# Paired attention in a two-block transformer kernel, with the gather schedule spread anew

## The chip, the cores and the metric

The kernel runs on one core of one Trainium2 chip. The metric is device time in microseconds for one execution of the whole program, as the median of three runs. Everything is in fp32. Engines are named as in the profile: PE is TensorE (PEld its weight load), DVE is VectorE, ACT is ScalarE, POOL is GpSimd, SP issues the weight transfers.

## The reference, cut to what matters

Two transformer blocks over 512 tokens (plus 16 meta tokens in the first) of width 1024. The first block has a latent attention (8 heads, q and k 96 wide, v 64) beside a retention branch, then an expert layer ("PEER"): per token 128 experts are chosen from 16384, their rows of `peer_u` are multiplied with the token and their rows of `peer_v` are summed with the resulting weights. The second block has a pooling branch beside an attention with 16 heads in 2 key groups and three branches per head, then an up/down MLP.

```python
# first block, per tile i of 128 queries
s = jnp.einsum('bhqd,bhkd->bhqk', qb, k) * scale
s = jnp.where(kpos[None, :] <= qpos[:, None], s, -jnp.inf)
o = jnp.einsum('bhqk,bhkd->bhqd', jax.nn.softmax(s, axis=-1), v)
# experts
act = jax.nn.gelu(jnp.einsum('td,tkd->tk', xt, peer_u[it]))
y = jnp.einsum('tk,tkd->td', gt * act, peer_v[it])
# second block, per head: compressed keys, selected blocks, window
o = gb[..., 0:1] * o_c + gb[..., 1:2] * o_s + gb[..., 2:3] * o_w
```

With 512 tokens the selection takes all blocks and the window covers everything, so both full branches are plain causal attention over `128 (t + 1)` keys for query tile t; the compressed branch has 15 keys after two tiles, 31 after four, with a mask of its own.

## The kernel before, in words

The 512 tokens are four tiles of 128 rows. Each block runs in two waves of two tiles: `first_wave` with run 0 (tiles 0, 1) and run 1 (tiles 2, 3), then `second_wave` with run 0 and run 1. Run by run the stages follow each other; a stage's tag with the run behind it is its name here. In the first block: n1 (norm), lat, nq, nkv, up, qk, tq, tk (transposes of q and k), the attention ma0 (run 0: tiles 0 and 1 in one stage) or ma2 and ma3 (run 1: tile 3 has 528 keys and a stage of its own), rp, tr, re, rn (retention), to (transposes of the attention's output), m1, mix, np, pq, and sel0 to sel3 (choice of the experts, VectorE work). In the second: n2, u, pool, q, kc, kv, cmp (the compressed keys), tq, tk, the attention na, to, m, out, n3, ff1, ff2, nf.

**Stages.** Each stage writes its instructions to all engines; an engine's queue is in order, and `Core.begin` makes each wait for the last results of the stage before. Weights stream through a ring of three 2 MB slabs (L236), loaded by SP in the order of `weight_plan`.

**Picks.** The 1024 expert rows per token (4 tiles x 128 experts x 2 tables) are 1024 gathers of 128 rows of 4 KB, issued by POOL (L304) into a ring of 8 buffers. VectorE uses each: a multiply-and-sum with the token for `peer_u` (L361), a scaled addition to `h` for `peer_v` (L367). They run behind other stages: the picks of tiles 0 and 1 behind run 1 of the first block, those of tiles 2 and 3 behind run 0 of the second. `SHARES` says how many picks each stage takes, `share` and `after` spread them over the stage's turns, and `use` (L344) emits them between VectorE's own instructions. At drain_0 the sum must reach 512, at the end 1024; what is left at nf is worked off before run 1 of the second block. `on_pe` (L76) could hand picks to TensorE and returns False.

**Attention** (`attention_stage`, L782). An item is one head of one query tile, for the second block one branch of one head. Per item: TensorE multiplies q with the keys (L833, contraction over 64 or 96 partitions) and adds the causal bias by a product of the identity with a bias table (L834), meta keys in L838; VectorE takes the negated maximum (L929); ScalarE takes the exponential with the row sum (L888); TensorE transposes the probabilities block by block (L873); ScalarE copies them to SBUF (L897, L900); TensorE multiplies them as the stationary operand with v, 64 columns moving (L863); VectorE scales the output by gate over row sum and adds the branches (L916, L918). Three scores are in flight (two in the 528-key stage). The token-major output is transposed afterwards by the stage "to". The queries of the second block are 64 partitions wide, `[HD, NH, width]`.

An fp32 matrix product appears in the trace as two records, an fp32 transpose as one. "64\*128" in a row is the shape of the stationary operand, contraction rows by columns; the form behind it is what moves.

## Time and profile before

| | us |
|---|---|
| median of 3 runs | 3428.84 (3423.63 to 3446.03) |
| the profiled execution | 3448.32, span 3447.0 |
| PE busy | 2413.4 (70%) |
| DVE busy | 1903.6 (55%) |
| POOL busy | 1311.0 (38%) |
| ACT busy | 431.7 (13%) |
| moved | 761.9 MB, of them 539.8 MB gathers |

The busy shares are averages over stages with different limits, so the table says little by itself. The slices (each a fortieth of the span, 86 us) show where which engine is full; a stretch with one engine full and the others not is that engine's. A granted clock of 1.0 is 2.4 GHz, 0.5 is 1.2 GHz.

### The profile page before, as it was taken

What the parts mean: (1) busy time and instruction counts of PE and PEld (TensorE: products, weight loads), DVE (VectorE), ACT (ScalarE), POOL (GpSimd) and SP (SyncE); (2) the same over time, 40 slices, a digit from 0 to 9 for tenths busy, and PEclk for the clock granted to TensorE, in tenths of its full rate; (3) what the DMA queues carried; (4) which work ended last, traced back from release to release, by engine and by line L of the source; (5) the groups of instructions that cost most, each with busy time, mean ns of one, the idle gap of its engine ahead of it and who ended that gap; (6) DMA issues with size and microseconds to landing.
All of it is one profiled execution on the core that took longest, in us unless ns stands there. A gap on an engine that the chain in (4) does not pass through costs nothing. (4 is left out here: it accounts for less than half of the span.)

```text
span 3447.0 us, 25459 instructions
## 1 busy us (share of the span) xinstructions
PE 2413.4 (70%) x8594; PEld 1672.6 (49%) x8594; DVE 1903.6 (55%) x3694; ACT 431.7 (13%) x1194; POOL 1311.0 (38%) x1041
## 2 busy tenths in 40 slices
PE   6998940356857633002739999499518999999998
PEld 3736730224525513001437668285215766678763
DVE  1412159878676678998779866766672222211100
ACT  1201000002101000000003220021000222220100
POOL 0000004677465877337678657654640000000000
PEclk9797975675667866555855559799859555569999
DMA  4221416798687999668899879999963100004342
GB/s 156 72 85 49 159 39 195 260 378 308 219 346 275 402 351 355 201 214 327 326 400 335 275 226 350 386 383 401 402 241 118 44 1 0 1 27 157 130 156 93
DMA packets 259169, 761.89 MB, mean 221 GB/s; under 512 B 22000, under 2 KB 28576, under 8 KB 258528
## 3 DMA queue, kind: packets, MB, share of 16 engines
q0 software_dynamic: 148416, 539.79, 42.9%
q1 hardware_dynamic: 107328, 215.88, 17.3%
q10 hardware_dynamic: 3296, 4.60, 0.4%
q8 instruction: 69, 1.13, 0.1%
q14 instruction: 60, 0.49, 0.0%
HBM read 758.10 MB, written 2.10 MB: 221 GB/s over the span
## 5 line engine op out<-in xcount | busy, mean ns | idle before, releaser
L304 POOL DMA_INDIRECT picks_rows<-peer_u_dram,expert x512 | 686.2, 1340 | 828.0 <-DVE expert L1439 522.6
L304 POOL DMA_INDIRECT picks_rows<-peer_v_dram,expert x512 | 617.3, 1206 | 413.6 <-DVE h L367 300.9
L367 DVE SCALAR_TENSOR_TENSOR h<-picks_rows,picks_weight,h 128x1024 f32<-128x1024 f32 x512 | 654.9, 1279 | 101.0 <-DMA picks_rows<-peer_v_dram,expert 80.9
L361 DVE CUSTOM_DVE_ANT_0 picks_rows<-picks_rows,xn 128x1024 f32<-128x1024 f32 x512 | 615.0, 1224 | 165.8 <-DMA picks_rows<-peer_u_dram,expert 161.9
L635 PE MATMUL psum<-identity_sb,n_scaled 128*128 128x128 f32 (+1 forms) x104 | 23.6, 411 | 399.8 <-DVE n_scaled L620 399.8
L445 PE MATMUL psum<-weight_ring,hnT 128*128 128x512 f32 (+4 forms) x576 | 236.3, 572 | 23.4 <-DMA weight_ring<-w_in_dram 11.9
L445 PE MATMUL psum<-xn,weight_ring 128*128 128x256 f32 x1024 | 222.9, 381 | 8.9 <-DVE xn L601 8.9
L1725 PE MATMUL psum<-weight_ring,aT 128*128 128x512 f32 x512 | 220.8, 593 | 3.2 <-DMA weight_ring<-w_ff_dram 1.3
L635 PEld LDWEIGHTS psum<-identity_sb,n_scaled 128*128 128x128 f32 (+1 forms) x104 | 20.2, 224 | 403.8 <-issue 362.8
L445 PEld LDWEIGHTS psum<-xn,weight_ring 128*128 128x128 f32 x1024 | 195.4, 191 | 36.3 <-issue 9.6
L929 DVE TENSOR_REDUCE na_negmax<-psum 128x1 f32<-128x15 f32 (+5 forms) x192 | 73.8, 384 | 239.4 <-PE psum L834 239.3
L833 PE MATMUL psum<-nsa_kT_sb,qT 64*128 64x128 f32 (+3 forms) x256 | 182.2, 813 | 0.0
L445 PEld LDWEIGHTS psum<-weight_ring,hnT 128*128 128x128 f32 (+1 forms) x576 | 105.8, 186 | 152.6 <-issue 138.3
L1725 PEld LDWEIGHTS psum<-weight_ring,aT 128*128 128x128 f32 x512 | 96.9, 190 | 126.3 <-issue 120.1
L863 PE MATMUL psum<-nsa_kv_sb,na_probsT 128*128 128x64 f32 x640 | 157.7, 413 | 0.2 <-DVE xn L918 0.2
L863 PEld LDWEIGHTS psum<-nsa_kv_sb,na_probsT 128*128 128x128 f32 x640 | 151.5, 333 | 0.3 <-issue 0.3
L445 PE MATMUL psum<-weight_ring,mergedT 128*128 128x512 f32 x256 | 116.1, 616 | 46.4 <-DVE mergedT L1190 46.4
L834 PEld LDWEIGHTS psum<-causal_sb,identity_sb 128*128 128x128 f32 x320 | 82.7, 309 | 123.3 <-issue 121.1
L1385 PE MATMUL psum<-keysT_sb,pqT 64*128 64x128 f32 x128 | 11.4, 347 | 175.0 <-DVE gates_sb L1445 174.1
L888 ACT ACTIVATE na_probs<-psum,na_negmax 128x15 f32<-128x15 f32 (+5 forms) x192 | 85.3, 444 | 347.7 <-DVE na_negmax L929 337.9
L873 PE MATMUL psum<-identity_sb,na_probs 128*128 128x128 f32 (+2 forms) x384 | 125.2, 430 | 0.7 <-ACT na_probs L888 0.7
L834 PE MATMUL psum<-causal_sb,identity_sb 128*128 128x128 f32 x320 | 120.2, 478 | 0.0
(332 smaller groups left out, 3260.8 us busy)
## 6 DMA issues: line engine op xcount, KB each, us to landing
weight_ring<-w_in_dram SPq DMA_DIRECT2D x36, 2048.0 KB, 17.7
weight_ring<-w_ff_dram SPq DMA_DIRECT2D x32, 2048.0 KB, 14.1
weight_ring<-w_ret_out_dram SPq DMA_DIRECT2D x4, 2048.0 KB, 7.9
weight_ring<-w_mix_out_dram SPq DMA_DIRECT2D x4, 2048.0 KB, 17.3
weight_ring<-w_peer_q_dram SPq DMA_DIRECT2D x4, 2048.0 KB, 13.2
picks_rows<-peer_u_dram,expert POOLq DMA_INDIRECT x512, 8.5
picks_rows<-peer_v_dram,expert POOLq DMA_INDIRECT x512, 6.2
weight_ring<-w_proj_nsa_dram SPq DMA_DIRECT2D x4, 2048.0 KB, 7.9
```

The lines of the kernel that those rows point to most:

```text
L304: pool.indirect_dma_start(out=self.rows[:, n % GATHERS, :], out_offset=None, in_=table, in_offset=bass.IndirectOffsetOnAxis(ap=self.expert ...
L361: ins = nc.vector.tensor_tensor_reduce(out=row, in0=row, in1=self.x[t], scale=1.0, scalar=0.0, op0=ALU.mult, op1=ALU.add, accum_out=self.d ...
L367: ins = nc.vector.scalar_tensor_tensor(out=h, in0=row, scalar=self.weight[:, t % 2, k:k + 1], in1=h, op0=ALU.mult, op1=ALU.add)
L445: mm = g.nc.tensor.matmul(g.psum[0:rows, n % BANKS, 0:cols], lhsT, rhs, start=(k == 0), stop=(k == len(pairs) - 1))
L635: mm = nc.tensor.transpose(g.psum[:, 2 * (t % 2) + c // 4, P * (c % 4):P * (c % 4) + rows], buffer(t)[0:rows, P * c:P * c + P], g.identity ...
L833: nc.tensor.matmul(scores(i)[:, at:end], it.q, it.kT, start=True, stop=False)
L834: return nc.tensor.matmul(scores(i)[:, end - it.bias.shape[1]:end], g.identity[:], it.bias, start=False, stop=True)
L863: mm = nc.tensor.matmul(values(j), probsT[0:keys, j % 2, P * m:P * m + P], v, start=(m == 0), stop=(m == last))
L873: mm = nc.tensor.transpose(turned(j, m, keys), probs[:, j % depth, col:col + keys], g.identity[:])
L888: nc.scalar.activation(probs[:, i % depth, 0:items[i].keys], scores(i), ACT.Exp, bias=negmax[:, i % 4:i % 4 + 1], accum_out=rowsum[:, i % ...
L929: nc.vector.tensor_reduce(negmax[:, i % 4:i % 4 + 1], scores(i), AX_X, ALU.max, negate=True).then_inc(s_max.sem, 1)
L1725: mm = nc.tensor.matmul(g.psum[:, n_tiles * b + t, :], aT[:, KT * k + i, P * t:P * t + P], w[:, i, :], start=(k == 0 and i == 0), stop=(k ...
```

## The change

The attention is done in steps of two items, a pair of heads. The q of the second block is stored `[P, NH // 2, width]`, so that even heads lie on partitions 0 to 63 and odd heads on 64 to 127; keys are stored twice, once for each half (`turn_twice`). The scores come negated (q is scaled by a negative factor); the mask is added in PSUM by the VectorE pass that finds the minimum, and the bias products go. The probabilities are normalised (and gated) before they are transposed. v is now the stationary operand, 64 columns wide, and the transposed probabilities move, 128 columns; the output lands transposed in PSUM, even heads on partitions 0 to 63 and odd ones on 64 to 127, and the three branches add up there. ScalarE copies one set of eight heads at a time. The stages "to" are gone. Four scores are in flight (two in the 528-key stage), and four buffers of probabilities. `SHARES` has new numbers. The mechanism for picks on TensorE is extended (`fold`, more calls of `picks.add`) and stays unused. Some stages have more turns: cmp six instead of three, ff2 sixteen instead of eight.

```diff
 SHARES = {
-    "sel1": 24, "n1_1": 14, "lat_1": 19, "nq_1": 9, "nkv_1": 10, "up_1": 19, "qk_1": 19, "tq_1": 5, "tk_1": 6, "ma2_1": 28,
-    "ma3_1": 28, "rp_1": 43, "tr_1": 7, "re_1": 19, "rn_1": 8, "to_1": 4, "m1_1": 71, "mix_1": 24, "np_1": 14, "pq_1": 28,
-    "sel2": 43, "sel3": 42, "drain_0": 28, "n22_0": 11, "u2_0": 11, "pool2_0": 9, "q2_0": 23, "kc2_0": 11, "kv2_0": 15,
-    "cmp2_0": 41, "tq2_0": 6, "tk2_0": 3, "na2_0": 119, "to2_0": 4, "m2_0": 56, "out2_0": 19, "n32_0": 11, "ff12_0": 82,
-    "ff22_0": 82, "nf2_0": 9}
+    "sel1": 24, "n1_1": 13, "lat_1": 13, "nq_1": 9, "nkv_1": 9, "up_1": 12, "qk_1": 16, "tq_1": 6, "tk_1": 5, "ma2_1": 26,
+    "ma3_1": 27, "rp_1": 35, "tr_1": 7, "re_1": 58, "rn_1": 9, "m1_1": 55, "mix_1": 18, "np_1": 22, "pq_1": 18, "sel2": 51,
+    "sel3": 51, "drain_0": 28, "n22_0": 15, "u2_0": 10, "pool2_0": 14, "q2_0": 20, "kc2_0": 11, "kv2_0": 20, "cmp2_0": 55,
+    "tq2_0": 10, "tk2_0": 4, "na2_0": 109, "m2_0": 62, "out2_0": 19, "n32_0": 15, "ff12_0": 67, "ff22_0": 66, "nf2_0": 15}
...
+def turn_twice(g, bank, columns, src, rows):
+
+    for part in (0, HD):
+        mm = g.nc.tensor.matmul(g.psum[part:part + HD, bank, columns], src, g.identity[0:rows, 0:rows], start=True, stop=True)
+    return mm
...
-def attention_stage(g, tag, items, head_dim, group):
+def attention_stage(g, tag, items, outputs):
...
         def values(i):
-            return g.psum[:, 5 + (i % 2 if two else 0), 0:head_dim]
-
-        def score(i):
-            it, (at, _) = items[i], starts(i)
-            end = at + it.kT.shape[1]
-            nc.tensor.matmul(scores(i)[:, at:end], it.q, it.kT, start=True, stop=False)
-            return nc.tensor.matmul(scores(i)[:, end - it.bias.shape[1]:end], g.identity[:], it.bias, start=False, stop=True)
...
+            it = items[i]
+            return g.psum[MV * it.part:MV * it.part + MV, 6 + it.set % 2, P * it.column:P * it.column + P]
+
+        def score(pe, s):
+            for i in pair(s):
+                it = items[i]
+                if i >= depth:
+
+                    pe.wait_ge(*s_exp.after(i - depth + 1))
...
+                mm = nc.tensor.matmul(scores(i)[:, 0:it.kT.shape[-1]], it.q, it.kT, start=True, stop=True)
...
+                mm.then_inc(s_scores.sem, 1)
+
+        def turn(pe, s):
+            for j in pair(s):
+                pe.wait_ge(*s_normed.after(j + 1))
+                if j >= 2:
+                    pe.wait_ge(*s_copied.after(j - 1))
+                for m, (at, keys, _) in enumerate(items[j].blocks):
+                    mm = nc.tensor.transpose(turned(j, m, keys), probs[:, j % 4, at:at + keys], g.identity[:])
+                mm.then_inc(s_turned.sem, 1)
+
+        def value(pe, s):
+            for j in pair(s):
+                it = items[j]
+                pe.wait_ge(*s_copied.after(j + 1))
...
+                for m, (_, keys, v) in enumerate(it.blocks):
+                    mm = nc.tensor.matmul(values(j), v, probsT[0:keys, j % 4, P * m:P * m + P], start=it.start and m == 0,
+                                          stop=it.stop and m == len(it.blocks) - 1)
+                mm.then_inc(s_values.sem, 1)
...
+            for s in range(steps + 2):
+                if wide:
+                    turn(pe, s - 1)
+                    score(pe, s)
+                else:
+                    score(pe, s)
+                    turn(pe, s - 1)
+                value(pe, s - 2)
...
         def vector(dve):
             g.begin(dve)
             link = linker(dve, s_link)
...
+            for s in range(steps):
+                for i in pair(s):
                     dve.wait_ge(*s_scores.after(i + 1))
-                    nc.vector.tensor_reduce(negmax[:, i % 4:i % 4 + 1], scores(i), AX_X, ALU.max, negate=True).then_inc(s_max.sem, 1)
...
+                    nc.vector.tensor_tensor_reduce(out=scores(i), in0=scores(i), in1=items[i].mask, scale=1.0, scalar=-LOWEST,
+                                                   op0=ALU.add, op1=ALU.min, accum_out=least[:, i % 8:i % 8 + 1]).then_inc(s_least.sem, 1)
+                g.picks.use(dve)
+                for i in pair(s):
+                    it, p = items[i], probs[:, i % 4, 0:items[i].keys]
+                    f = factor[:, i % 8:i % 8 + 1]
+                    dve.wait_ge(*s_exp.after(i + 1))
+                    if it.seen is not None:
+                        nc.vector.tensor_tensor(p, p, it.seen, ALU.mult)
+                    link(nc.vector.reciprocal(f, rowsum[:, i % 8:i % 8 + 1]))
+                    if it.gate is None:
+                        ins = nc.vector.tensor_scalar(p, p, f, None, ALU.mult)
+                    else:
+                        ins = nc.vector.tensor_scalar(p, p, f, it.gate, ALU.mult, ALU.mult)
+                    ins.then_inc(s_normed.sem, 1)
                 g.picks.use(dve)
```

ScalarE runs, per step, the exponentials of step s (scale -1, bias the minimum) and the copies of step s - 1, in the wide stage the copies first.

## Rows read from the trace of the kernel before

**Rows 1.** The page, part 2: PE's busy tenths and clock in 40 slices.
```profile
PE   6998940356857633002739999499518999999998
...
PEclk9797975675667866555855559799859555569999
```

**Rows 2.** Busy time by stretch; columns: us, PE, PEld, DVE, ACT, POOL, clock, DMA, GB/s.
```profile
118.00:173.00 55.00, 52.72 (x221) 45.91 (x218) 11.98 (x42) 17.30 (x66) 0.00 (x0) 0.53 0.03 12
...
616.00:783.80 167.80, 79.51 (x226) 43.70 (x226) 138.55 (x250) 19.25 (x45) 123.14 (x90) 0.71 0.93 347
783.80:916.70 132.90, 88.22 (x313) 68.83 (x313) 95.14 (x118) 26.10 (x70) 84.98 (x68) 0.53 0.79 274
...
977.30:1077.50 100.20, 36.09 (x152) 26.58 (x152) 77.46 (x110) 12.58 (x37) 61.22 (x49) 0.52 0.77 284
1077.50:1323.00 245.50, 165.54 (x658) 129.33 (x660) 174.03 (x294) 16.30 (x34) 188.52 (x132) 0.82 0.97 363
...
1591.00:1815.60 224.60, 124.84 (x466) 89.89 (x466) 177.39 (x326) 19.08 (x37) 164.93 (x126) 0.68 0.93 353
1815.60:1922.00 106.40, 102.67 (x341) 76.17 (x342) 102.06 (x210) 32.62 (x153) 86.58 (x66) 0.51 0.91 326
1922.00:2055.00 133.00, 131.38 (x428) 90.36 (x427) 102.64 (x205) 37.36 (x141) 77.45 (x61) 0.50 0.76 243
...
2238.50:2463.60 225.10, 222.86 (x768) 146.55 (x768) 142.58 (x159) 26.28 (x66) 121.24 (x114) 0.99 1.02 393
2463.60:2563.60 100.00, 0.01 (x1) 0.00 (x0) 82.06 (x69) 3.78 (x6) 64.50 (x54) 0.52 0.91 350
2702.30:2867.00 164.70, 163.78 (x516) 108.97 (x515) 39.89 (x141) 47.67 (x146) 0.00 (x0) 0.51 0.00 1
2867.00:3072.80 205.80, 205.41 (x638) 135.75 (x637) 45.24 (x148) 54.12 (x144) 0.00 (x0) 0.50 0.00 1
```

**Rows 3.** Order of time, PE in na2_1, tile 3; start, length, instruction.
```profile
3009.71 2.07 PE L833 MATMUL psum<-nsa_kT_sb,qT 64*128 64x512 f32 x2
3011.71 0.80 PE L834 MATMUL psum<-causal_sb,identity_sb 128*128 128x128 f32 x2
3012.30 1.81 PE L863 MATMUL psum<-nsa_kv_sb,na_probsT 128*128 128x64 f32 x8
```

**Rows 4.** Order of time, PE in the retention of run 0.
```profile
270.11 0.79 PE L1022 MATMUL psum<-retention_state,re_rqx 64*128 64x128 f32 x2
270.83 0.79 PE L1021 MATMUL psum<-picks_rows,re_decayed 128*128 128x128 f32 x2
...
272.28 1.97 PE L1025 MATMUL psum<-picks_rows 128*64 128x128 f32 x16
274.18 1.71 PE L1009 MATMUL psum<-xn 64*128 64x128 f32 x16
```

**Rows 5.** Busy time by stretch: the q transposes ahead of na2_1, and behind.
```profile
2695.00:2698.70 3.70, 3.70 (x18) 3.00 (x19) 0.81 (x2) 1.18 (x2) 0.00 (x0) 0.50 1.04 399
2698.90:2702.00 3.10, 2.28 (x22) 2.04 (x21) 1.72 (x3) 1.18 (x2) 0.00 (x0) 1.00 0.00 1
```

**Rows 6.** Groups by line and form; count, busy us, mean ns, idle before.
```profile
L361 DVE CUSTOM_DVE_ANT_0 picks_rows<-picks_rows,xn 128x1024 f32<-128x1024 f32 x512 | 615.0, 1224 | 165.8 <-DMA picks_rows<-peer_u_dram,expert 161.9 <-DVE k_cmpT_sb L1581 0.2
...
L361 DVE DVE_READ_ACCUMULATOR2_ANT picks_dots<- 128x1 f32 x512 | 41.4, 81 | 0.0
L888 ACT ACTIVATION_READ_ACCUMULATOR na_probs<-psum,na_negmax 128x1 f32 x192 | 37.0, 193 | 0.0
...
L929 DVE TENSOR_REDUCE na_negmax<-psum 128x1 f32<-128x512 f32 x32 | 22.1, 691 | 100.2 <-PE psum L834 100.2
L888 ACT ACTIVATE na_probs<-psum,na_negmax 128x512 f32<-128x512 f32 x32 | 22.0, 687 | 92.0 <-DVE na_negmax L929 92.0
...
L897 ACT COPY na_probsT<-psum 128x512 f32<-128x512 f32 x32 | 18.7, 585 | 35.4 <-PE psum L873 35.4
...
L620 DVE TENSOR_SCALAR n_scaled<-h,n_inverse 128x1024 f32<-128x1024 f32 x12 | 8.9, 754 | 0.2
```

More of the change, by code:

```diff
@@ L158, with __init__ @@
 class Item:
-    def __init__(self, q, kT, bias, v, meta, seen, gates, out, add):
-        self.q, self.kT, self.bias, self.v, self.meta = q, kT, bias, v, meta
-        self.seen, self.gates, self.out, self.add = seen, gates, out, add
-        self.keys = kT.shape[1] + (0 if meta is None else META)
+    def __init__(self, q, kT, mask, v, meta, seen, gate, place, ends):
+        self.q, self.kT, self.mask, self.seen, self.gate, self.meta = q, kT, mask, seen, gate, meta
+        self.set, self.part, self.column = place
+        self.start, self.stop = ends
+        n = kT.shape[-1]
+        self.keys = n + (0 if meta is None else META)
+        self.blocks = [(P * m, min(P, n - P * m), x) for m, x in enumerate(v)]
+        if meta is not None:
+            self.blocks.append((n, META, meta[1]))
 def linker(eng, signal):
@@ L383, in add_to @@
             at = self.number[n] - 1
-            mine = [m for m in range(PICKS) if on_pe(m)]
-            if k == mine[0] and t:
-                pe.wait_ge(self.sum_added, 2 * t)
+            mine = [m for m in range(PICKS) if on_pe(t, m)]
+            if k == mine[0] and self.sums[t]:
+                pe.wait_ge(self.sum_added, self.sums[t])
             pe.wait_ge(self.landed[n % GATHERS], 16 * (n // GATHERS + 1))
@@ L630, in tensor @@
             for t, (_, rows, _) in enumerate(sources):
+                g.picks.add(pe, t)
                 pe.wait_ge(*s_scaled.after(t + 1))
@@ L675, in tensor @@
             mm.then_inc(s_turned.sem, 1)
+            g.picks.add(pe, n + 1)
         g.picks.add(pe)
@@ new lines, in copies @@
+        def copies(act, s):
+            for j in pair(s):
+                act.wait_ge(*s_turned.after(j + 1))
+                if j >= 4:
+                    act.wait_ge(*s_values.after(j - 3))
+                full = [m for m, (_, keys, _) in enumerate(items[j].blocks) if m < 4 and keys == P]
+                if full:
+                    ins = nc.scalar.copy(probsT[:, j % 4, 0:P * len(full)], g.psum[:, 4 + j % 2, 0:P * len(full)])
+                for m, (_, keys, _) in enumerate(items[j].blocks):
+                    if m not in full:
+                        ins = nc.scalar.copy(probsT[0:keys, j % 4, P * m:P * m + P], turned(j, m, keys))
+                ins.then_inc(s_copied.sem, 1)
@@ L1101, in tensor @@
         for t in range(n):
+            g.picks.add(pe, t)
             pe.wait_ge(*s_gated.after(t + 1))
@@ L1540, in tensor @@
                     mm.then_inc(g.w.products_done, 1)
+                    g.picks.add(pe, 2 * x + j + 1)
             for x in range(2):
@@ L1569, in vector @@
             link = linker(dve, s_link)
-            g.picks.use(dve)
+            for _ in range(4):
+                g.picks.use(dve)
             dve.wait_ge(*s_out.after(1))
@@ L1633, in tensor @@
             g.begin(pe)
+            g.picks.add(pe, n)
             pe.wait_ge(*s_diff.after(1))
```

288 lines of the change are left out of this document (119 added, 169 removed).

## The prediction, made before the result was known

> **What bounds the kernel now.** I read the page first, then cut the span into stages with the view of busy time by stretch, then looked at TensorE alone inside the attention.
>
> The page [rows 1] shows two kinds of stretch. In slices 7 to 29 TensorE has gaps, down to nothing: here the 1024 expert gathers ("picks") run behind the other work. After it TensorE carries the time at 9 tenths, and in slices 31 to 35, the last attention (na2_1), its clock is at 0.5.
>
> The stretches [rows 2] give the terms. na2_1 lasts 164.7 + 205.8 = 370.5 us; TensorE is busy 369.2 of them, VectorE 85, ScalarE 102, DMA nothing: pure TensorE time at 1.2 GHz. The first attention (ma0_0, 55 us) is the same in small: 52.7 busy, clock 0.53. The others lie among the picks. In ma2_1 and ma3_1 (132.9 us) nothing is full (TensorE 88, VectorE 95, 274 GB/s): engines wait for one another in turn. In na2_0 (106.4 + 133 us) TensorE is full; VectorE is full in the first half, 103 of 133 in the second. Stages that stream weights move 347 to 393 GB/s, so picks there are paid in bytes. After the last product of that wave 100 us pass with TensorE idle and VectorE working off 54 picks.
>
> **The change, na2_1.** Before, one head of a full branch at 512 keys [rows 3] costs: score 2.00 us (start to start: two fp32 records and a change of shape), mask product 0.59, values 8 records, transposes 4 records. A record of 128 columns or a 128-column stationary goes every 0.213 (1.81 for 8, with 0.1 of tail), so 1.7 and, with a change, some 1.0. About 5.3 us, two heads 10.6. The compressed branch (31 keys) adds some 2.1 per head: 205.8 / 16 = 12.9 per head in all.
>
> The mask products go: VectorE adds the mask in the pass that finds the extreme. The two heads of a pair take score rows 0 to 63 and 64 to 127. The trace has such products: 16 records on alternating row halves took 1.71 us, and 16 with alternating output halves 1.97, so about 0.11 each, half of 0.213 [rows 4]. Two heads' scores are then worth one: 1.7. Transposes stay, 8 x 0.213 = 1.7. Values: v becomes a 64-column stationary and 128 columns move; each head's records are issued in a row on one half, so nothing overlaps: 16 x 0.213 = 3.4. A change of shape costs about 0.30: two 128-row records, then two 64-row ones start 0.72 apart [rows 4] against 0.43. The new step has three changes for two heads, the old one four.
>
> The Trainium skill (TensorEngine Tiling (Array Packing), Key Properties) says that changing the tiling mode drains TensorE; the trace agrees with its 0.30. The change from 128 to 64 columns before the values is what the rule holds against this edit; without it the step would be 0.3 shorter.
>
> At 1.2 GHz: 1.7 + 1.7 + 3.4 + 3 x 0.3 = 7.7 us for two heads. At 384 keys, three quarters of the records: 1.3 + 1.3 + 2.6 + 0.9 = 6.1. Compressed: 0.1 + 0.4 + 0.4 + 3 x 0.3 = 1.9 per pair against 4.2. A pair of heads: 2 x 7.7 + 1.9 = 17.3, and 2 x 6.1 + 1.9 = 14.1; eight of each make 251 us against 370.5: **-120**.
>
> *The clock.* The q transposes ahead of na2_1, back to back and busy all of their stretch at 0.50, were followed by 1.00 [rows 5]. The attention behind them, as busy, had 0.50 to 0.51 [rows 2]: there the shape changes after every two to twelve records. The new step has 24 records in a run (8 transposes, 16 values) with one change among them, 5.4 of 7.7 us. I count that nearer to the first than to the second and take 2.4 GHz. Streaming halves, 6.8 to 3.4; a change is taken at 0.2 (an estimate, between half of 0.30 and all): 4.0 us, at 384 keys 3.2, a pair of heads about 9.1 and 7.5. Now the other engines count [rows 6]: from the end of a score, extreme 0.77, exponentials 2 x (0.69 + 0.19), reciprocal 0.17, normalising 0.45, with gaps 3.4 us; VectorE takes the next step's extreme only behind that. A short step between full ones exposes 1 us per pair. (10.1 + 8.5) x 8 = 149, and 11 for stretches at the low clock: **160, -210**. ScalarE's own floor is 4 x (0.69 + 0.19 + 0.59) + 1.6 = 7.5 per pair, VectorE's 7.9.
>
> *VectorE's prices.* The mask-and-extreme pass reads and writes PSUM. Nearest rows [rows 6]: reduction of 512 from PSUM, 691 ns; multiply-and-sum of 1024 in SBUF, 1224, the same rate. I take 0.69 + 0.08 for reading the sum. Lower end 0.69; upper end twice, 1.4, if the write-back doesn't overlap. Normalising in SBUF: 0.75 for 1024 gives some 0.45 for 512; upper end 0.69. The 0.28 per head for the output goes, and with it the adding of the branches: TensorE accumulates them. New is that VectorE waits for the exponentials inside each step; behind it stand the second half of the step's picks and the next extreme. In the pick zone the first half of the picks (over 1.28 us) lies in front and covers it; in na2_1 it is the 3.4 us chain above.
>
> *ma0_0*: 16 mask products (16 x 0.43 = 7) go; longer runs may lift the clock, then 55 becomes some 33. **-20**, lower end -7. *Output turns*: the output is born transposed; the two exposed stages are 4 + 2 us; q transposes halve, k's are done twice: **-8** in all. *At nothing*: `on_pe` stays False, so `add`, `fold` and the sums issue nothing; the finer turns in cmp and ff2 only order the same picks.
>
> **The pick zone.** A pick costs VectorE 1.28 us (1224 ns and the reading of the sum [rows 6]) and 0.52 MB (128 rows of 4 KB) wherever it lies. Counts before are gathers issued, the POOL column of [rows 2]; after, sums of SHARES.
> - n1 to tk: 90 to 13+13+9+9+12+16+6+5 = 83, at 1.6 each: -11.
> - ma2, ma3: 53 x 1.29 = 68, VectorE's own 21 (16 heads at 1.2 to 1.4), 5 of gaps: 95 against 133. The stage was no engine's; with TensorE at some 80 it becomes VectorE's: -38.
> - re, rn: 67 plus some 12 that rp can't take, 79 against 49: 79 x 1.29 + 14 own + 4 = 120 against 100: +20.
> - m1 to pq: 55+18+22+18 = 113 against 132, in bytes at 363 GB/s, 1.44 each: -27.
> - n2 to tk of the second block: 126 to 159: 79 + 17 MB at 393 GB/s = 245 against 225: +20.
> - na2_0: TensorE's work falls to some 140 us, so VectorE bounds: 109 x 1.29 = 141 and 96 heads at 0.9 to 1.1 = 92, so 233 against 239, with 18 picks fewer: -6. The clock doesn't matter here.
> - m to n3: about 88 to 62+19+15 = 96: +5.
> - Up, down, tail: 168 to 67+66+15 = 148, at 1.6 to 1.85 (100 / 54): -34.
>
> Sum -71. Some of it will come back as waits at the joints: **-65**.
>
> **Sum.** -210 - 20 - 8 - 65 = -303. The profiled execution took 3448 us (span 3447), so 3145. The median of the runs is 3428.8, 19 lower, so the same sum gives 3126; rounded 3130.
>
> **Rivals.**
> *The clock stays at 1.2 GHz.* For it: every long stretch of attention so far shows 0.50 to 0.53 [rows 2]. -120 - 7 - 8 - 65 = -200: **3230**. By the Trainium skill (TensorE: Matmul & The Clock Gate, Part 4) transposes don't count as busy for the clock; then the eight in the new step would not help and this would be the case. Against it, here transposes alone were followed by 1.00 [rows 5].
> *The PSUM pass is the price.* At twice, a head costs 0.2 to 0.7 us more: 28 in na2_0, 10 in ma, and VectorE passes TensorE in na2_1 at 11.8 and 10.3 per pair, +30. Together +68: **3200**.
> *The spread gives nothing.* The gains of ma and the tail are eaten by re and by n2 to tk: +60, **3190**. For it: byte-bound stages stay byte-bound.
> *Slower.* The mask-and-extreme pass lies on VectorE's path in na2_0 and ma (112 heads), and in na2_1 once that is bound (96). Each us above my price is then 208 us. From 1.45 us extra, three times the dearest row, the gain is gone and beyond it the kernel is slower. No row is near it.
>
> **How the numbers follow.** Forecast 0.5, clock 0.25, PSUM pass 0.12, spread 0.1, slower 0.03. The forecast's own range is 3090 to 3175 (zone -65 +/- 30, na2_1 150 to 175). The full one reaches the clock rival with 30 us less of the zone's gain: 3090 to 3260. A measurement of this kernel can tell about 1% from no change: faster 0.96, same 0.02, slower 0.02.
>
> **What would show it.** na2_1 near 160 us with a granted clock over 0.8; 250 at 0.5 says the rival. Scores of a pair starting together, 16 value records in a run. ma2 + ma3 near 95 us with VectorE over 90% busy. na2_0 near 235, VectorE full, TensorE below 70%. The tail after the down products below 80. The forecast is wrong if the pass over 512 columns takes over 1 us, if the row halves go one after the other, or if the whole tail comes back in n2 to tk.

## The result

The changed kernel takes 3173.7 us (median of four, 3154.0 to 3178.7); the kernel before, timed beside it, 3427.7 (3423.6 to 3446.0). The ratio is 0.924, with a 95% interval of 0.919 to 0.929. The profiled execution took 3176 us, its span is 3174.6. Forecast were 3130 us and a range of 3090 to 3260, so the time lies inside it, at the upper end of the forecast's own range (3090 to 3175): faster by 254 us where the sum said 303.

The page of the kernel after, part 2: TensorE's busy tenths and clock in 40 slices, to be held against [rows 1].

```profile
PE   5997980056673784100166156875997298899998
...
PEclk9796995577685896655586555796999686999999
```

The slices with 9 tenths at clock 0.5 near the end are gone; the middle still has its gaps.

Busy time by stretch, after (columns as in [rows 2]). In this order: ma0_0; n1 to tk; ma2 and ma3; re and rn; m1 to pq; sel2, sel3 and drain; n2 to tk of the second block; na2_0; m to n3; up and down products; the tail behind them; na2_1, and its two tiles.

```profile
119.80:166.90 47.10, 43.96 (x185) 30.15 (x184) 14.18 (x65) 16.54 (x68) 0.00 (x0) 0.60 0.03 10
609.00:747.30 138.30, 79.09 (x226) 42.95 (x226) 117.61 (x214) 19.68 (x44) 97.97 (x72) 0.75 0.91 336
747.30:870.00 122.70, 67.17 (x275) 46.41 (x275) 93.96 (x157) 27.22 (x72) 93.04 (x64) 0.64 0.85 292
927.00:1055.40 128.40, 36.12 (x161) 26.79 (x161) 116.22 (x148) 14.45 (x40) 96.45 (x78) 0.53 0.92 340
1055.40:1281.60 226.20, 163.81 (x658) 129.33 (x658) 155.52 (x267) 14.27 (x31) 168.03 (x121) 0.84 0.98 371
1281.60:1558.00 276.40, 5.80 (x64) 5.34 (x64) 261.89 (x551) 6.01 (x10) 153.03 (x130) 0.52 0.77 264
1558.00:1812.00 254.00, 122.88 (x480) 91.09 (x480) 208.76 (x352) 16.63 (x31) 182.15 (x149) 0.65 0.95 362
1812.00:2026.00 214.00, 121.88 (x578) 63.35 (x576) 206.85 (x546) 61.33 (x294) 174.50 (x118) 0.51 0.85 291
2026.00:2216.00 190.00, 133.52 (x528) 102.74 (x528) 131.00 (x230) 11.42 (x24) 138.18 (x94) 0.83 0.94 361
2216.00:2443.00 227.00, 224.27 (x768) 147.76 (x768) 145.40 (x136) 27.21 (x66) 179.43 (x118) 0.99 1.02 393
2443.00:2508.50 65.50, 0.03 (x1) 0.00 (x0) 48.69 (x42) 3.78 (x6) 29.14 (x28) 0.53 0.89 341
...
2652.00:2806.50 154.50, 134.09 (x960) 88.11 (x960) 101.86 (x417) 88.22 (x293) 0.00 (x0) 0.90 0.01 1
2652.00:2722.00 70.00, 60.37 (x406) 37.86 (x406) 47.36 (x208) 39.65 (x143) 0.00 (x0) 0.85 0.00 1
2722.00:2806.00 84.00, 73.66 (x554) 50.25 (x554) 54.51 (x210) 48.17 (x150) 0.00 (x0) 0.94 0.01 1
```

Against the kernel before:

| stretch | before, us | after, us | change | forecast |
|---|---|---|---|---|
| ma0_0 | 55 | 47.1 | -8 | -20 |
| n1 to tk | 167.8 | 138.3 | -29 | -11 |
| ma2, ma3 | 132.9 | 122.7 | -10 | -38 |
| re, rn | 100.2 | 128.4 | +28 | +20 |
| m1 to pq | 245.5 | 226.2 | -19 | -27 |
| sel2, sel3, drain | 268 | 276.4 | +8 | 0 |
| n2 to tk, second block | 224.6 | 254.0 | +29 | +20 |
| na2_0 | 239.4 | 214.0 | -25 | -6 |
| m to n3 | 183.5 | 190.0 | +6 | +5 |
| up, down, tail | 325 | 292.5 | -33 | -34 |
| na2_1 | 370.5 | 154.5 | -216 | -210 |

The pick zone as a whole gave 48 us where 65 were forecast (a small stage between the attention and the retention gave 4). The front of the second block's last wave, n2 to tk ahead of na2_1, became 5 us longer. Turning q and k takes 7.3 us of TensorE there instead of 6.6; of the rest, 3 us are one product of 64 records that is the same in both kernels and ran at a clock of 0.82 instead of 1.00. Measured from the first score to the last value product, as the lines of the runs below are, na2_1 takes 369 us before and 153.5 after.

The step of na2_1 in order of time, after, TensorE alone, tile 3 (start, length, instruction; idle time in brackets), against [rows 3]:

```profile
2740.65 1.12 PE L872 MATMUL psum<-identity_sb,na_probs 128*128 128x128 f32 x8 [1.18 <-ACT na_probsT L915]
2741.70 1.58 PE L883 MATMUL psum<-na_probsT,nsa_kv_sb 128*64 128x128 f32 x16
2743.21 1.13 PE L861 MATMUL psum<-nsa_kT_sb,qT 64*128 64x512 f32 x4
2744.27 0.41 PE L872 MATMUL psum<-identity_sb,na_probs 128*31 128x128 f32 x2
```

Two heads' scores, four records of 512 columns, take 1.13 us; before, one head's two took 2.07, at half the clock. Sixteen value records take 1.58. Together with the eight transposes a full step of two heads takes TensorE 3.6 us; the 1.18 in brackets is idle time in front of a step.

Groups by line and form in na2_1, after (count, busy us, mean ns, idle before), against [rows 6]:

```profile
L905 ACT ACTIVATE na_probs<-psum,na_least 128x512 f32<-128x512 f32 x32 | 21.7, 682 | 31.8 <-DVE na_least L943 31.8
L943 DVE CUSTOM_DVE_ANT_0 psum<-psum,mask_sb 128x512 f32<-128x512 f32 x32 | 21.5, 713 | 16.5 <-PE psum L861 16.5
...
L956 DVE TENSOR_SCALAR na_probs<-na_probs,na_factor,branch_gates 128x512 f32<-128x512 f32 x32 | 17.5, 546 | 1.2
```

The new pass that adds the mask and takes the extreme, in place in PSUM, costs 713 ns for 512 columns, where the plain reduction cost 691.

### The profile page after: what moved, and what is told of

It is laid out like the page before. It is cut to its first block and busy times, and to the rows that moved or that the text cites. A ratio compares the mean times of both kernels' runs of the same rounds, so it can differ in the third digit from the quotient of the medians.

```text
span 3174.6 us, 24361 instructions
## 1 busy us (share of the span) xinstructions
PE 2029.1 (64%) x8126; PEld 1373.0 (43%) x8126; DVE 1932.4 (61%) x3993; ACT 405.7 (13%) x1191; POOL 1387.9 (44%) x1041
## 5 line engine op out<-in xcount | busy, mean ns | idle before, releaser
L313 POOL DMA_INDIRECT picks_rows<-peer_u_dram,expert x512 | 704.3, 1376 | 797.4 <-DVE expert L1463 515.9
L313 POOL DMA_INDIRECT picks_rows<-peer_v_dram,expert x512 | 676.1, 1320 | 312.2 <-DVE h L378 183.0
L463 PE MATMUL psum<-xn,weight_ring 128*128 128x256 f32 x1024 | 224.3, 383 | 11.6 <-DVE xn L619 11.6
L872 PE MATMUL psum<-identity_sb,na_probs 128*128 128x128 f32 (+2 forms) x384 | 89.3, 344 | 110.4 <-DVE na_probs L956 91.7
L1179 PE MATMUL psum<-hnT,weight_ring 128*128 128x256 f32 x512 | 116.4, 390 | 5.0 <-ACT xn L1138 5.0
L872 PEld LDWEIGHTS psum<-identity_sb,na_probs 128*128 128x128 f32 (+2 forms) x384 | 45.5, 152 | 168.7 <-DVE na_probs L956 156.1
L1179 PE MATMUL psum<-h2T,weight_ring 128*128 128x256 f32 x512 | 114.2, 385 | 1.3 <-ACT xn L934 1.3
L943 DVE CUSTOM_DVE_ANT_0 psum<-psum,mask_sb 128x128 f32<-128x128 f32 (+7 forms) x160 | 76.4, 514 | 60.7 <-PE psum L863 31.3
L1179 PE MATMUL psum<-xn,weight_ring 128*128 128x256 f32 x512 | 111.9, 380 | 0.5 <-DMA weight_ring<-w_proj_nsa_dram 0.5
L905 ACT ACTIVATE na_probs<-psum,na_least 128x15 f32<-128x15 f32 (+5 forms) x192 | 83.7, 441 | 199.4 <-DVE na_least L943 196.7
L1179 PEld LDWEIGHTS psum<-hnT,weight_ring 128*128 128x128 f32 x512 | 100.5, 197 | 20.0 <-ACT xn L1138 5.8
```

The source lines that it names most:

```text
L313: pool.indirect_dma_start(out=self.rows[:, n % GATHERS, :], out_offset=None, in_=table, in_offset=bass.IndirectOffsetOnAxis(ap=self.expert ...
L463: mm = g.nc.tensor.matmul(g.psum[0:rows, n % BANKS, 0:cols], lhsT, rhs, start=(k == 0), stop=(k == len(pairs) - 1))
L872: mm = nc.tensor.transpose(turned(j, m, keys), probs[:, j % 4, at:at + keys], g.identity[:])
L905: nc.scalar.activation(probs[:, i % 4, 0:items[i].keys], scores(i), ACT.Exp, bias=least[:, i % 8:i % 8 + 1], scale=-1.0, accum_out=rowsum[ ...
L943: nc.vector.tensor_tensor_reduce(out=scores(i), in0=scores(i), in1=items[i].mask, scale=1.0, scalar=-LOWEST, op0=ALU.add, op1=ALU.min, acc ...
L1179: mm = nc.tensor.matmul(g.psum[0:rows, n % BANKS, 0:cols], lhsT, rhs, start=(k == 0), stop=(k == len(pairs) - 1))
```

## The experiments

The clock is the granted clock of the stretch named.

**What the spread is worth: `a_oldshares` and `b_newshares`.** The one is the changed kernel with the old table, the other the kernel before with the new one.

```diff
-SHARES = {"sel1": 24, "n1_1": 13, ..., "re_1": 58, ..., "na2_0": 109, "m2_0": 62, ...}
+SHARES = {"sel1": 24, "n1_1": 14, ..., "re_1": 19, ..., "na2_0": 119, "m2_0": 60, ...}
```

> The changed kernel with the table of picks of the kernel before (the two counts whose stages no longer turn an output are added to the stages behind them); nothing else differs. Theory: the spread is worth the part of the zone's 49 us that the faster attention does not give by itself. The tail after the last down product goes back from 65 to some 100 us (+34), n2 to tk back from 254 to 225 and re, rn from 128 to 100 (-57), n1 to tk from 138 to 168 (+29), m1 to pq +19; na2_0 with 119 instead of 109 picks +10; ma2 and ma3 are 28 + 28, unchanged. Sum about +20: 3195 us. Rival 1, the spread gives nothing: 3174. Rival 2, all 49 us of the zone come from the spread: 3222.

Measured: 3191.1 us (3179.8 to 3194.2), ratio 0.930 (0.928 to 0.932).

> The kernel before with the new table of picks, attention as before. Theory: the spread needs the new attention, because na2_0 is TensorE's there (its 109 instead of 119 picks bring nothing while TensorE is full) and ma2, ma3 are an exchange of waits: -33 in up, down and tail, -29 in n1 to tk, -19 in m1 to pq, +28 in re and rn, +29 in n2 to tk, +8 in sel2, sel3: -16, so 3412 of 3428 us, within 1%. Rival 1, the spread brings most of the zone's 49 us by itself: 3380. Rival 2, nothing at all: 3428.

Measured: 3427.4 us, ratio 0.998 (0.996 to 1.000).

So the spread is worth about 17 us on the new attention (the intervals of 0.919 to 0.929 and 0.928 to 0.932 overlap slightly), as its theory said, and 8 us on the old (3435.3 for the kernel before beside it; by the interval 1 to 15). Rival 1 falls in the second run; between its theory (-16) and "nothing at all" it does not decide, and whether the spread is worth more on the new attention than on the old is not shown. Of the zone's 48 us some 30 come from the new attention alone. The second run holds a surprise in ma0_0, whose instructions are those of the kernel before (first line the kernel before, second line this run):

```profile
122.00:172.00 50.00, 49.65 (x197) 43.32 (x198) 9.90 (x36) 15.30 (x64) 0.00 (x0) 0.50 0.00 1
124.00:152.00 28.00, 27.50 (x198) 24.53 (x198) 9.89 (x36) 15.24 (x64) 0.00 (x0) 1.00 0.01 1
```

In this profile the stage ran at 1.00 and TensorE was busy for 27.5 us; in the profile of before the same records took 49.7 us at 0.50. The same stream of instructions can fall on either level, and some 20 us of the difference between two single profiles can be of this kind. The high level is the rare one here: in all 13 other profiles of this document, of either kernel or a variant, the stretch from 124 to 152 us has 0.50 to 0.54.

**What the halves are worth: `a_samehead`.**

```diff
-for branch in range(3):
-    for h in (h0, h0 + 1):
+for pairs in (((0, h0), (0, h0 + 1)), ((1, h0), (2, h0)), ((1, h0 + 1), (2, h0 + 1))):
+    for branch, h in pairs:
```

> The changed kernel with the items of the second block's attention in another order: a full step holds two branches of one head instead of one branch of two heads. Same instructions, shapes and counts; only the two items of a step now lie on the same half of TensorE's rows (scores) and of its output columns (values), so nothing can run side by side. Theory: the side-by-side running is worth, at 2.4 GHz, a second score (0.43 to 0.55 us) and some of the values' overlap per full step; 16 steps per tile, 32 in na2_1: a step goes up by 0.9 to 1.2 us, na2_1 from 154 to 185 us, na2_0 little because VectorE is full: about 3207 us. Rival 1, the halves run one after another anyway and the gain is the mask's and the clock's: 3174. Rival 2, without the side-by-side records the clock stays at 1.2 GHz: na2_1 near 280, 3300 us.

Measured: 3180.0 us (3178.2 to 3182.9), ratio 0.927 (0.925 to 0.929). In order of time, TensorE of this run:

```profile
2742.50 1.96 PE L883 MATMUL psum<-na_probsT,nsa_kv_sb 128*64 128x128 f32 x16
2744.39 1.98 PE L861 MATMUL psum<-nsa_kT_sb,qT 64*128 64x512 f32 x4
```

The scores went from 1.13 to 1.98 us and the values from 1.58 to 1.96: 1.23 us per full step, as expected, or 39 us of TensorE's work in 32 steps. But na2_1 grew by 14 us only:

```profile
2641.50:2809.40 167.90, 159.31 (x960) 105.70 (x960) 107.92 (x416) 90.94 (x292) 0.00 (x0) 0.97 0.00 1
```

TensorE's idle time fell from 20 to 9 us and its clock rose from 0.90 to 0.97: part of the extra work lay in gaps, part was given back by the clock. So in the changed kernel TensorE doesn't set the step alone, and running side by side brings 14 of 39 us. Neither rival holds, and the theory holds for the step alone: it had 31 us for the stage and 33 for the kernel, 14 and 6 came.

**Whether the mask products held the clock down: `b_nomask`.** The kernel before without them.

```diff
-nc.tensor.matmul(scores(i)[:, at:end], it.q, it.kT, start=True, stop=False)
-return nc.tensor.matmul(scores(i)[:, end - it.bias.shape[1]:end], g.identity[:], it.bias, start=False, stop=True)
+return nc.tensor.matmul(scores(i)[:, at:end], it.q, it.kT, start=True, stop=True)
```

> The kernel before without its mask products (the causal and the block mask are left out, nothing else). Theory: the mask products are 64 of 0.59 us in na2_1 and 16 of 0.43 in ma0_0, and the clock stays at 0.50: na2_1 from 370 to 325, ma0_0 to 48, the rest less: 3365 us. Rival, it is the mask product in the middle of the step that keeps the clock low: with it gone the clock rises and na2_1 falls under 230, 3250 us or less.

Measured: 3373.8 us, ratio 0.983 (0.980 to 0.986). Its na2_1:

```profile
2678.40:2997.60 319.20, 318.10 (x960) 201.68 (x960) 84.06 (x287) 101.48 (x289) 0.00 (x0) 0.50 0.00 1
```

The mask products are worth 50 us there, and the clock stays at 0.50. The theory holds. How the 216 us of na2_1 divide can be estimated from busy time times clock. Before, TensorE was busy for 369 us at 0.50 to 0.51 [rows 2]; after, for 134 at 0.90, which at the clock of before would be about 240. So some 130 us come from the instructions (50 of them the mask; the halves save 39 us at full clock, 78 at half) and some 85 from the clock, less 20 us of new gaps.

**Whether the long runs hold the clock up: `a_split`.**

```diff
-turn(pe, s - 1)
-value(pe, s - 2)
+for only in range(2):
+    turn(pe, s - 1, only)
+    value(pe, s - 2, only)
```

> The changed kernel with TensorE's order inside a step of the second block's attention cut up: turn of one head, values of one head, turn of the other, values of the other, instead of both turns and then both values. So the runs of like records are half as long, the shape changes five times instead of three times per step, and the values of the two heads no longer stand behind one another; the records and the other engines' work are the same. Theory (the long runs of like records keep the clock up): the clock in na2_1 falls back to 0.5 and na2_1 goes from 154 to 250 or more: 3270 us. Rival (the clock is up for another reason, the runs don't matter): two more changes of 0.2 to 0.3 us in 32 full steps and the lost overlap, +15 to +25: 3195 us.

Measured: 3180.8 us, ratio 0.924 (0.917 to 0.931). Its na2_1:

```profile
2645.90:2807.30 161.40, 150.54 (x960) 95.64 (x960) 102.89 (x416) 89.46 (x292) 0.00 (x0) 0.97 0.00 1
```

With runs half as long and five changes of shape per step the clock is 0.97. (The edit, like those of `a_early` and `a_early2` below and of the runs built on them, also reaches ma0 and ma2 of the first block, whose stages share this code; only the 528-key stage keeps its order.) The theory falls, and it was the prediction's own argument for the clock. The two changes and the lost overlap cost TensorE 16 us of work and the stage 8.

**Whether the form of the value products does it: `a_oldvalues`.**

```diff
-mm = nc.tensor.matmul(values(j), v, probsT[0:keys, j % 4, P * m:P * m + P], start=it.start and m == 0,
+ops = (v, probsT[0:keys, j % 4, P * m:P * m + P])
+mm = nc.tensor.matmul(values(j), *(ops[::-1] if tag[:2] == "na" else ops), start=it.start and m == 0,
...
```

> The changed kernel with the value products of the second block's attention in their old form: the probabilities (128 columns) are the stationary operand and 64 columns of v stream, instead of v (64 columns) stationary and 128 columns streaming. As many records in the same runs, into as much of PSUM; the copy out of PSUM is as large (its layout, and with it the output of the attention, is not the reference's). Theory A (it is the doubled stream of the value records that keeps the clock up): the clock falls to 0.5 in na2_1, which takes 250 us or more: 3270 us. Theory B (it is the runs and the paired scores): the clock stays over 0.8; a record with a 128-column stationary costs as much as one with 128 columns streaming, only the overlap of two heads' values goes and a wait at three joints of output sets comes: na2_1 +10 to +20, 3190 us.

Measured: 3216.2 us (3200.5 and 3231.8), ratio 0.934 (0.926 to 0.943). Its na2_1:

```profile
2650.30:2859.50 209.20, 194.78 (x960) 150.30 (x960) 103.20 (x416) 89.38 (x292) 0.00 (x0) 0.65 0.00 1
```

The clock fell to 0.65, between the theories and nearer to A. This profile is of the slower of two executions that lie 31 us apart, so the level is that of one profile. Because TensorE also had gaps here (14 us) and waits at the joints of the output sets, the form was tried once more with fewer gaps, below.

**What sets the step: `a_early` and `a_early2`.** First VectorE's order alone.

```diff
-for s in range(steps):
-    for i in pair(s):
+for s in range(steps + 1):
+    for i in (pair(s) if wide else pair(s + 1) if s else range(0, 4)):
```

> The changed kernel with VectorE's order turned in the second block's attention: it takes the extreme of the next step's two scores before it normalises this step's probabilities. Same instructions. Theory (the chain score, extreme, exponentials, normalising, turn sets the step of na2_1, and TensorE waits 17 us for ScalarE's copies and some for VectorE): the exponentials of the next step start up to 1 us earlier, TensorE's gaps shrink from 20 to under 10 us: na2_1 154 to 142, na2_0 unchanged because VectorE is full: 3162 us. Rival (TensorE's own records set the step): 3174, nothing changes.

Measured: 3339.2 us, ratio 0.972 (0.966 to 0.978), 165 us slower than the changed kernel. Waits in its na2_1 (engine, line, waited for: us, times, longest):

```profile
DVE psum L943 <- PE psum L861: 162.0, 48, 5.9
ACT na_probs L905 <- DVE na_least L943: 125.7, 46, 4.7
...
PE psum L872 <- DVE na_probs L957: 78.4, 57, 2.1
```

VectorE waits for the next step's scores before it normalises; TensorE turns only what is normalised, and its next scores stand behind that turn and the values: a ring through all three engines. na2_0, forecast unchanged, grew from 200 to 245 us; na2_1 took 270 us, and with TensorE idle for 79 of them its clock fell as well:

```profile
2693.80:2963.50 269.70, 190.68 (x960) 124.60 (x960) 97.05 (x416) 98.01 (x292) 0.00 (x0) 0.66 0.00 1
```

Then with TensorE's scores a step ahead:

```diff
-score(pe, s)
+if s == 0:
+    score(pe, 0)
+score(pe, s + 1)
 turn(pe, s - 1)
```

> The changed kernel with two turns of order in the second block's attention, same instructions: VectorE takes the extreme of the next step's scores before it normalises this step's probabilities (as in the run before), and TensorE now makes each step's scores one step earlier, so that this extreme has nothing to wait for. Theory (in the first try TensorE made the next scores behind the values, which hung on VectorE: a ring through all engines; with the scores a step ahead the ring is open, and TensorE's own records set the step): na2_1 from 154 to 135 to 140, with TensorE over 95% busy and the clock near 1; na2_0 unchanged: 3158 us. Rival (what cost in the first try was VectorE's order itself): na2_1 over 200, 3230 us or more.

Measured: 3137.1 us (3134.7 to 3145.4), ratio 0.914 (0.911 to 0.916). Its na2_1:

```profile
2637.80:2766.30 128.50, 125.88 (x960) 81.52 (x960) 95.64 (x416) 92.14 (x292) 0.00 (x0) 0.96 0.01 1
```

128.5 us, even less than expected: TensorE is busy 98% and sets the stage. The theory holds, with 25 us where 14 to 19 were forecast: 17 of them are TensorE's gaps, which the chain score, extreme, exponentials, normalising had caused, and 8 are busy time, with the clock at 0.96 instead of 0.90. The kernel gained 37 us; na2_0 took 200 us as before, and where the other 12 lie is open.

**The value form again, with few gaps: `a_early2_oldvalues`.** The edits of `a_oldvalues` and `a_early2` together.

> The order of the run a_early2, where TensorE is busy 126 of 128.5 us of na2_1 at a clock of 0.96, with the value products in their old form (128 columns of probabilities stationary, 64 columns of v streaming; the layout of the attention's output is not the reference's). Question: in the run a_oldvalues the clock had fallen to 0.65, but there TensorE also had gaps and three joint waits. Theory (the form of the value records does it, not the gaps): the clock stays under 0.75 although TensorE is never idle, na2_1 175 us or more, 3185 us. Rival (the gaps did it): clock over 0.9, na2_1 128.5 plus 32 full steps at 0.5 and the joints, 145 to 150, 3157 us.

Measured: 3182.0 us, ratio 0.926 (0.919 to 0.932). Its na2_1, whole and in three stretches of it:

```profile
2654.60:2808.70 154.10, 148.36 (x960) 114.17 (x960) 95.78 (x416) 91.62 (x292) 0.00 (x0) 0.87 0.00 1
2675.00:2695.00 20.00, 18.85 (x142) 14.47 (x140) 15.10 (x71) 14.48 (x52) 0.00 (x0) 0.99 0.01 2
2695.50:2724.50 29.00, 29.00 (x118) 21.93 (x118) 11.85 (x55) 10.39 (x36) 0.00 (x0) 0.50 0.00 1
2725.00:2808.70 83.70, 80.97 (x600) 63.69 (x598) 55.09 (x228) 53.74 (x162) 0.00 (x0) 1.00 0.01 1
```

Neither theory holds as it was put. The same steps in the old form run at 0.99, then for 29 us at 0.50 although TensorE is never idle, then at 1.00 to the end although it is idle for 2.7 us. Within one tile (the next begins at 2731) neither the form of the records nor the gaps tell which level comes.

**Who sets na2_0: `a_actnorm`.** ScalarE does the 96 normalising passes (in its step s those of step s - 1), VectorE one reciprocal and one product with the gates for two heads.

```diff
+if by_act:
+    nc.scalar.activation(p, p, ACT.Copy, scale=factor[:, i % 8:i % 8 + 1])
...
+    link(nc.vector.reciprocal(factor[:, two], rowsum[:, two]))
+    link(nc.vector.tensor_tensor(factor[:, two], factor[:, two], items[i - 1].pair_gate, ALU.mult))
```

> The changed kernel with the normalising of na2_0 (96 heads) moved from VectorE to ScalarE: VectorE makes one reciprocal and one product with the gates for two heads (2 x 0.16 us) instead of two reciprocals and two normalising passes (2 x 0.16 + 2 x 0.35), ScalarE does the 96 passes. Theory (VectorE sets na2_0: 207 of 214 us busy): VectorE is freed of 48 x 0.7 = 33 us, na2_0 goes from 214 to 181 with the same 109 picks, the stages after it start earlier with the same picks: 3141 us. Rival (the gathers set it: they start 1.81 us apart): na2_0 stays over 205, 3170.

Measured: 3139.2 us (3130.4 to 3156.8), ratio 0.911 (0.906 to 0.917). Its na2_0, from where TensorE goes on behind its first scores (in the changed kernel that stretch has 200 us):

```profile
1834.00:2009.00 175.00, 109.37 (x568) 60.49 (x568) 169.07 (x432) 91.72 (x383) 139.37 (x109) 0.54 0.91 324
```

25 us fewer in the stage, where 33 were forecast, and 35 in the kernel as forecast, with a wide interval; the profiled execution, the slowest of four, has 19 fewer. VectorE set it, not the gathers: as many picks (108) now take 25 us less.

**What ma2 and ma3 cost without picks: `a_manopicks`.**

```diff
-"ma2_1": 26, "ma3_1": 27, ..., "drain_0": 28
+"ma2_1": 0, "ma3_1": 0, ..., "drain_0": 81
```

> The changed kernel with no picks in ma2_1 and ma3_1; their 53 are done in drain_0 before the second block. Question: how much of these two stages is the attention itself. Theory (prediction's sum: VectorE full, 53 x 1.29 of picks, the attention's own waits hidden behind them): without picks the two stages take what TensorE needs, some 60 of 123 us, and the drain grows by 53 x 1.3 = 69: 3180 us. Rival (the waits of the engines for one another set them, and picks lie beside them for little): the two stages still take 90 us or more, 3210 us.

Measured: 3190.6 us, ratio 0.929 (0.926 to 0.931). The two stages without picks:

```profile
747.30:819.00 71.70, 55.04 (x297) 37.73 (x296) 32.07 (x84) 26.32 (x72) 18.24 (x12) 0.81 0.37 144
763.00:819.00 56.00, 48.20 (x264) 32.83 (x264) 20.38 (x66) 23.40 (x66) 4.67 (x5) 0.84 0.18 72
```

The first line is the stretch that was 122.7 us. Its first 16 us are not the attention's: VectorE still works off picks of the stage in front, and TensorE, its first scores done, stands for 10. The second line starts with the first extreme. From there the attention takes 56.0 us, TensorE busy for 48 of them and VectorE for 20; in the changed kernel, with the 53 picks of the two stages, the same part takes 110:

```profile
761.00:871.10 110.10, 63.26 (x264) 43.77 (x264) 84.23 (x141) 26.10 (x70) 81.35 (x58) 0.64 0.83 279
```

The theory holds, the rival falls: without picks the stages take little more than TensorE's work. The 53 picks add 54 us, hardly less than their own 64 us of VectorE, so only a little of them is hidden in the attention's waits. The clock is 0.84 without them and 0.64 with them.

**Both improvements: `a_best`.**

> Both improvements together: the normalising of na2_0 on ScalarE, and the order of the run a_early2 in the second block's attention. If both theories hold, -35 in na2_0 and the stages behind it and -16 in na2_1: 3122 us. If only the first holds, 3139. Rival: a second ring appears in na2_0, where ScalarE normalises ahead of the next exponentials: 3150 or more.

Measured: 3124.4 us (3113.7 to 3128.9), ratio 0.909 (0.907 to 0.911). Its na2_1, and its na2_0 from where TensorE goes on behind its first scores:

```profile
2614.90:2743.40 128.50, 125.62 (x960) 81.42 (x960) 95.58 (x416) 92.07 (x292) 0.00 (x0) 0.96 0.00 1
1814.90:1990.60 175.70, 113.14 (x568) 62.79 (x568) 169.52 (x432) 87.72 (x385) 141.85 (x110) 0.53 0.92 323
```

Both gains stand side by side. It beats both kernels: 49 us below the changed one and 309 below the one before, timed beside it (3433.8).

## Why the prediction was right, and where its terms were off

The profiled execution was to take 3145 us and took 3176. Of these 31 us, 17 are the pick zone, 12 ma0_0 and 8 the output turns, and na2_1 gave 6 more than forecast. The largest term, two thirds of the sum, was right. Part of the agreement is luck: the zone's 17 us are misses of 28 on one side and of 18 and 19 on the other, with some of 8 and 9 beside them.

*na2_1, -210 forecast, -216 measured.* A pair of heads was to take 10.1 us at 512 keys and 8.5 at 384; 84 and 70 us for eight pairs each are 10.5 and 8.8. The parts hold: scores side by side (1.13 for two heads), no mask products (50 us by `b_nomask`), clock over 0.8. Two terms were off and cancelled. "Nothing overlaps" in the values is wrong: the last records of one head run beside the first of the next, 1.58 us for 16 against 1.96 on one half (`a_samehead`). And the chain through VectorE exposed more than the 1 us per pair, 16 us in all: 25 us came back once it was hidden (`a_early2`), 8 of them by the clock. The division into instructions and clock holds too: 120 and 90 forecast, some 130 and 85 measured.

*The clock.* The forecast took 2.4 GHz, and 0.90 came. The reason given for it, long runs with few changes of shape, fell with `a_split` (0.97), so this part of the sum came out by luck as far as its reason goes. The rule of the Trainium skill (TensorE: Matmul & The Clock Gate, Part 4), that a transpose doesn't count as busy in the same way, would have made 3230 us; this trace doesn't bear out that result, since 0.90 came with eight transposes in each full step. The level of na2_1 is no accident of one profile: with unchanged instructions it has 0.90, 0.90 and 0.92 in three (the changed kernel, `a_actnorm`, `a_oldshares`), 0.96 in `a_early2` and `a_best`, and 0.50 in the kernel before and `b_newshares`.

What sets it stays open. Within the new form it goes with TensorE's gaps: 0.96 with 3 us of them, 0.97 with 9 and with 11, 0.90 with 20, 0.66 with 79. The old form had less, 0.65 with 14 us of gaps and 0.87 with 6, in one profile each. But the kernel before had next to no gap (1.3 us) and 0.50, with its mask products and without (`b_nomask`), and `a_early2_oldvalues` ran the same steps at 1.00 and, for 29 us without a gap, at 0.50. So neither form nor gaps are shown as the cause. The old value form with one head at a time, as before, wasn't tried by itself.

*ma0_0, -20 forecast, -8 measured.* The size was off, and it is the clock again: 0.60 in the stretch, not 1.00, and no profile of a kernel with the new attention has over 0.54 in its middle. That its level is no property of the instructions alone is shown by `b_newshares`.

*Output turns, -8 forecast, nothing measured.* The stretches outside the table add up to the same time as before: the part behind na2_1 became 6 us shorter, the front of the last wave 5 longer and the front of the kernel 1.

*VectorE's prices.* The mask-and-extreme pass was priced at 0.77 with the read of its result. Measured are 713 ns against 691 for the old reduction: the rival of a pass twice as dear falls. Normalising: 0.45 forecast for 512, 546 ns measured.

*na2_0, -6 forecast, -25 measured.* The mechanism was right: VectorE is busy 207 of 214 us. Its own work was mis-sized at 92 us for 96 heads, 0.96 each. In order of time, VectorE in na2_0, after:

```profile
1879.76 0.29 DVE L943 CUSTOM_DVE_ANT_0 psum<-psum,mask_sb 128x128 f32<-128x128 f32 x1
1879.97 0.14 DVE L943 DVE_READ_ACCUMULATOR2_ANT na_least<- 128x1 f32 x1
1879.97 0.33 DVE L943 CUSTOM_DVE_ANT_0 psum<-psum,mask_sb 128x128 f32<-128x128 f32 x1
1880.22 0.14 DVE L943 DVE_READ_ACCUMULATOR2_ANT na_least<- 128x1 f32 x1
1880.22 1.28 DVE L378 SCALAR_TENSOR_TENSOR h<-picks_rows,picks_weight,h 128x1024 f32<-128x1024 f32 x1
1881.42 0.16 DVE L952 RECIPROCAL na_factor<-na_rowsum 128x1 f32<-128x1 f32 x1
```

The durations of the two passes and their reads add up to 0.90 us, yet the pick starts 0.46 after the first: the next instruction starts before the last has ended. The pick too, 1.28 long, is followed after 1.20. From 1826 to 2026 VectorE is busy for 194 us and there are 96 + 12 picks; at 1.20 to 1.28 from start to start they are 130 to 138, which leaves 56 to 65 us for 96 heads, 0.6 to 0.7 each. The durations of those heads' instructions add up to 93 us, what the prediction had: its rows were right, and adding them up was the mistake. The picks were off the other way: 118 gathers lie in the whole stretch, not 109.

*ma2 and ma3, -38 forecast, -10 measured.* This is the step that failed. VectorE was to be over 90% busy in 95 us: 68 for 53 picks, 21 of its own, 5 of gaps. It is busy 94 of 122.7, 77%. Two things were left out. The stretch starts with 14 us in which VectorE works off nine picks of the stage in front before it takes the first extreme, while TensorE stands for 14.3; the kernel before has the like (11.2), and the prediction set its 95 against a stretch that holds it. Behind that come 110 us, busy 84 (89 forecast) but idle 26 and not 5: 10 for gathers that had not landed, 9 for scores, 6.3 of them at the joint of the two stages, and the rest in small pieces. Where VectorE works off a row of picks, the gathers don't keep up. VectorE in ma2, after:

```profile
780.86 1.23 DVE L372 CUSTOM_DVE_ANT_0 picks_rows<-picks_rows,xn 128x1024 f32<-128x1024 f32 x1 [0.78 <-DMA picks_rows<-peer_u_dram,expert]
...
782.99 1.23 DVE L372 CUSTOM_DVE_ANT_0 picks_rows<-picks_rows,xn 128x1024 f32<-128x1024 f32 x1 [0.91 <-DMA picks_rows<-peer_u_dram,expert]
...
785.13 1.23 DVE L372 CUSTOM_DVE_ANT_0 picks_rows<-picks_rows,xn 128x1024 f32<-128x1024 f32 x1 [0.90 <-DMA picks_rows<-peer_u_dram,expert]
```

They start 2.1 us apart, 0.8 to 0.9 of it waiting for a gather that has not landed; meanwhile TensorE and ScalarE stand, because the next extreme, with the exponentials and the turn that hang on it, comes behind these picks. The waits of the whole stretch show both:

```profile
PE psum L872 <- DVE ma_probs L954: 53.7, 8, 14.3
...
DVE picks_rows L372 <- DMA picks_rows<-peer_u_dram,expert: 12.9, 16, 1.0
```

*The rest of the zone.* n1 to tk: the price of 1.6 us per pick was right, the count wrong. The prediction held 90 gathers of the trace before against 83 of the new table; the two are not the same measure. The trace after has 72, so 18 fewer, as many as the table itself took out (101 to 83), and 18 x 1.6 = 29 is what was measured. The same slip with the other sign is in m1 to pq, where 113 were expected and 121 came: 8 us less of a gain. re and rn (+28) and n2 to tk (+29) took more than forecast by 8 and 9. For n2 to tk there is a slip in the sum: its 159 picks are 83 MB and not 79, and 83 + 17 MB at 393 GB/s are 255 us. That 254 were measured is chance, since only 149 gathers lay in the stretch and it moved 362 GB/s. The stages sel2, sel3 and the drain took 8 that had been put at nothing though their counts had risen by 17. Up, down and tail (-33) came as forecast, the tail with 65.5 us.

*Rivals.* "The spread gives nothing" (3190) is nearest in time, but for another reason: `a_oldshares` gives the spread some 17 us, and what was missing is in ma2, ma3 and ma0_0. The slower rival needed 1.45 us extra per pass; nothing near it came.

## What to carry to other kernels

Where several engines pass a tile round in turn, see that each engine's order lets the next step's input be made before this step's output is awaited: one such order cost 165 us and its mended form gained 37, with the same instructions. Price small VectorE instructions from start to start, not by the sum of their durations, and move those of the full engine to one that has room (35 us here). A stretch between two stages holds more than its own share of the work: count what really lies in it, and what one engine still has to finish from the stage in front, before adding up one engine's work.

## What the runs showed of the hardware

- The same stream (ma0_0 of the kernel before) ran at 1.00 in one profile and at 0.50 in another, TensorE busy for 27.5 and 49.7 us.
- With the same instructions na2_1 ran at 0.96 with 2.6 us idle of 128.5 (`a_early2`) and at 0.66 with 79 idle of 269.7 (`a_early`). A busy engine did not keep the high level by itself: the kernel before had 0.50 with 1.3 us idle of 370.5, and a stretch of 29 us without a gap in `a_early2_oldvalues` had 0.50 between stretches at 0.99 and 1.00.
- Two fp32 score products of 512 columns on different row halves take 1.13 us at full clock (`after`), on the same half 1.98 (`a_samehead`); sixteen value records on two output halves 1.58 when issued half after half, 1.96 on one half.
- Durations of small VectorE instructions overlap: two passes over 128 columns of PSUM and their reads last 0.90 us together and take 0.46.
- A VectorE pass that reads and writes PSUM in place costs what a plain reduction from PSUM costs: 713 against 691 ns for 512 columns.
